# The chunked recurrence with its inverse in two halves and the turned inverse made by transposes

## The reference, cut to what matters

```python
def wkv7_scan(state0, r, w, k, v, a_vec, b_vec, reverse):
    def step(S, inp):
        r_t, w_t, k_t, v_t, a_t, b_t = inp
        sa = jnp.einsum('bhij,bhj->bhi', S, a_t)
        S = (S * w_t[:, :, None, :] + sa[..., None] * b_t[:, :, None, :]
             + v_t[..., None] * k_t[:, :, None, :])
        return S, jnp.einsum('bhij,bhj->bhi', S, r_t)
```

## Time and profile before

| | before |
|---|---|
| median of 3 runs | 2858.52 us (2855.38 to 2859.93) |
| profiled execution | 2863.22 us |
| its span, first to last instruction | 2861.4 us |
| PE busy, of the span | 2508.4 us (88%) |
| DVE busy | 1637.7 us (57%) |
| ACT busy | 1215.2 us (42%) |
| POOL busy | 426.4 us (15%) |
| mean granted TensorE clock | 0.930 |

### The profile page before, as it was taken

How to read it: one execution, slowest core, us unless ns; L and a number is a source line. 1 busy time by engine, 2 the same in 40 slices (tenths; PEclk the granted TensorE clock), 3 DMA queues, 4 the chain that set the end, 5 groups by cost and what they waited for, 6 DMA issues and landing times.

```text
span 2861.4 us, 55427 instructions
## 1 busy us (share of the span) xinstructions
PE 2508.4 (88%) x23264; PEld 1945.2 (68%) x23264; DVE 1637.7 (57%) x2360; ACT 1215.2 (42%) x1740; POOL 426.4 (15%) x412
## 2 busy tenths in 40 slices
PE   6979889999978779997888887899977889988996
PEld 5745577787857436785888765777766656767774
DVE  3655535555442274445566564588965355548895
ACT  2433333222231216424333324278864247446784
POOL 1010001000010020002455401122220030012221
PEclk9978989999999779998999988999988899999997
DMA  4246922222211000100000031199863100017995
GB/s 176 89 154 254 351 87 96 96 88 97 93 61 45 25 0 1 78 16 5 2 0 0 10 139 61 68 385 378 339 263 133 66 1 2 25 70 286 355 345 199
DMA packets 63892, 353.33 MB, mean 123 GB/s; under 512 B 15329, under 2 KB 15345, under 8 KB 27248
## 3 DMA queue, kind: packets, MB, share of 16 engines
q1 hardware_dynamic: 41792, 292.60, 26.9%
q0 software_dynamic: 21936, 58.50, 5.5%
HBM read 344.91 MB, written 36.70 MB: 133 GB/s over the span
## 4 chain that ended last, share of the span: by engine, by line
PE 72%; DVE 8%; ACT 5%; issue 4%; PEld 3%; DVEq 3%; DMA 2%; POOL 1%; POOLq 1%; ACTq 1%; PEldq 1%
PE psum L642 13%; PE psum L436 12%; PE psum L3271 9%; PE psum L3293 4%; PE psum L1187 4%; PE psum L1827 3%; PE psum L1206 3%; PE psum L1197 3%; PE psum L2882 2%; PEld psum L436 2%; PE psum L2232 2%; PE psum L1733 2%; PE psum L2211 1%; PE psum L3236 1%; PE psum L1045 1%
## 5 line engine op out<-in xcount | busy, mean ns | idle before, releaser
L436 PE MATMUL psum<-arena_r 128*128 128x512 f32 (+1 forms) x976 | 312.3, 361 | 4.3 <-DVE weight_slots_r L462 4.2
L642 PE MATMUL psum<-arena_r 128*128 128x512 f32 x704 | 250.8, 397 | 10.8 <-issue 4.0
L436 PE MATMUL psum<-arena_r,weight_slots_r 128*128 128x512 f32 (+1 forms) x696 | 249.1, 358 | 0.0
L457 ACT ACTIVATE arena_r<-weight_slots 128x1024 fp32r<-128x1024 f32 x73 | 76.4, 1057 | 334.5 <-PE psum L436 251.1
L642 PE MATMUL psum<-arena_r,weight_slots_r 128*128 128x512 f32 x528 | 209.1, 396 | 0.0
L436 PEld LDWEIGHTS psum<-arena_r 128*128 128x128 f32 x976 | 179.3, 190 | 36.0 <-issue 4.3
L436 PE MATMUL psum<-h_t_r,arena_r 128*128 128x512 f32 (+1 forms) x528 | 192.7, 365 | 0.0
L3225 DVE TENSOR_TENSOR weight_slots_r<-weight_slots,arena_r 128x2048 fp32r<-128x2048 f32 x78 | 177.6, 2290 | 20.1 <-ACT arena_r L3220 19.7
L3225 DVE TENSOR_TENSOR weight_slots_r<-weight_slots,h_t_r 128x2048 fp32r<-128x2048 f32 x72 | 163.9, 2290 | 20.9 <-ACT h_t_r L3220 20.8
L642 PEld LDWEIGHTS psum<-arena_r 128*128 128x128 f32 x704 | 133.8, 190 | 45.6 <-issue 13.6
L1271 DVE TENSOR_REDUCE stat<-psum 128x1 f32<-128x768 f32 (+1 forms) x112 | 98.7, 881 | 108.1 <-PE psum L1187 107.9
(11 more groups left out here) (469 smaller groups left out, 5485.0 us busy)
## 6 DMA issues: line engine op xcount, KB each, us to landing
weight_slots<-in_weights SPq DMA_DIRECT2D x277, 1024.0 KB, 6.8
arena<-y_rows POOLq DMA_DIRECT2D x20, 512.0 KB, 7.9
h_rows<-arena POOLq DMA_DIRECT2D x10, 512.0 KB, 2.9
x_keep<-x_t POOLq DMA_DIRECT2D x1, 3072.0 KB, 9.0
x_t<-x_keep POOLq DMA_DIRECT2D x2, 1536.0 KB, 8.6
x_t<-in_x POOLq DMA_DIRECT2D x1, 2048.0 KB, 9.8
out_x<-x_t SPq DMA_DIRECT2D x1, 2048.0 KB, 7.2
arena<-in_toe POOLq DMA_DIRECT2D x1, 1792.0 KB, 7.3
```

The lines of the kernel that those rows point to most:

```text
L436: last = self.nc.tensor.matmul(self.bank(n), w[:, kt, :], self.operand(part, kt, a, b), start=(i == 0), stop=(i == len(passes) - 1))
L642: last = nc.tensor.matmul(bank, w(p, k), x(q, k), start=(k == j == 0), stop=(k == n - 1 and j == 2))
```

## The change

The inverse is made in two halves, units c = 0, 1 and c = 2, 3, each with two banks of its own (4 and 5, 6 and 7). At each level and for each half PE first transposes x as it stands, two 128x128 transposes into the second half of the half's first bank (`turned`), and then makes the half product as before. ACT copies both out, the product to t1 and the transpose to xt, 128x256 each. Then come the products beside, then the growing of the first and of the second half; DVE adds each half to x. xt is no longer grown from level to level, only in the last level, where the growing is turned. So the turned set of grams, its preset and its mask (`up`) are gone.

The transposes of v, b and k and the key products move from the step's start into the levels: `key_grams` beside level 0, the last grams and the transposes of b and v beside level 1, `w_from_state` beside level 2, `w_from_keys` in one part and the transposes of k beside level 3, `y_from_state` beside level 4. ACT's copies of those transposes move behind levels 1 and 3. On DVE `reading` moves behind `low`, `removal` ahead of the adds of level 3, `new_keys` behind level 2, and the last mask behind level 1. On POOL `keyed` stands one level later. The units also lie in another, plainer arrangement, in which `w_from_state` and `y_from_state` and the last growing have their results in the same half as their operands.

The diff, cut to PE's levels, ACT, DVE and POOL:

```diff
-            wait("more_factors", n)
-            turn(6, w.vc)
-            turn(7, w.bt)
-            wait("y_added", n, -1)
-            turn(0, w.kt)
-            wait("masked", n, 2)
-            wait("read", n)
-            key_grams().then_inc(self.sem("more_grams"), 1)
-            for lv in range(self.LEVELS):
-                half(lv)
...
+            def half(lv, h):
+                for c in (2 * h, 2 * h + 1):
+                    for e, d in corners:
+                        last = t.matmul(into(4 + 2 * h, 0, d, c % 2, e), self.by_token(w.lo[lv % 2], c, d, e), self.by_token(w.x, c, d, e),
+                                        start=True, stop=True)
...
+            def turned(h):
+                for c in (0, 1):
+                    at = (2 * h + c) * P
+                    t.transpose(self.turned_bank(h)[:, c * P:(c + 1) * P], w.x[:, at:at + P], ident)
+            def grow(lv, h):
+                wait("level_half_copied", n, 2 * lv + h)
...
+            def beside(lv):
                 if lv == 0:
+                    wait("more_factors", n)
+                    wait("read", n)
+                    wait("state", n, -2)
+                    key_grams().then_inc(self.sem("more_grams"), 1)
+                if lv == 1:
+                    wait("y_added", n, -1)
+                    last_gram().then_inc(self.sem("more_grams"), 1)
+                    wait("more_masked", n, 0)
+                    turn(3, w.bt)
+                    turn(2, w.vc)
+                if lv == 2:
+                    w_from_state()
+                if lv == 3:
+                    w_from_keys()
+                    turn(2, w.kt)
+                if lv == last_lv:
+                    y_from_state()
+            for lv in range(self.LEVELS):
+                wait("level_blocks", n, lv)
+                for h in self.HALVES:
+                    if lv:
+                        wait("level_added", n, 2 * lv - 2 + h)
+                    turned(h)
+                    half(lv, h)
+                beside(lv)
+                for h in self.HALVES:
+                    grow(lv, h)
...
+        def half_copied(n, lv, h):
+            act.wait_ge(*self.at("level_half", n, 2 * lv + h))
+            s.activation(self.four(w.t1[:, self.cols(h)]), self.chain(h), ACT.Copy)
+            s.activation(w.xt[:, self.cols(h)], self.turned_bank(h), ACT.Copy).then_inc(self.sem("level_half_copied"), 1)
...
+        def grown(n, lv, h):
+            dve.wait_ge(*self.at("level_summed", n, 2 * lv + h))
+            if lv < self.LEVELS - 1:
+                x = self.four(w.x[:, self.cols(h)])
+                last = v.tensor_tensor(out=x, in0=x, in1=self.chain(h), op=ALU.add)
+            else:
+                x = w.xt[:, self.cols(h)]
+                last = v.tensor_tensor(out=x, in0=x, in1=self.turned_bank(h), op=ALU.add)
+            last.then_inc(self.sem("level_added"), 1)
...
+            key_masks(n)
             for lv in range(self.LEVELS):
+                if lv == 3 and more:
+                    removal(n + 1)
+                for h in self.HALVES:
+                    grown(n, lv, h)
+                if lv == 1:
+                    last_mask(n)
+                if lv == 2 and more:
+                    new_keys(n + 1)
                 if lv == 3 and more:
                     replacement(n + 1)
             if more:
...
                 low(n + 1)
-                new_keys(n + 1)
-                up(n + 1)
+                reading(n + 1)
             state(n)
...
-                if lv == 2 and n + 1 < self.STEPS:
+                if lv == 3 and n + 1 < self.STEPS:
                     keyed(n + 1)
             if n + 1 < self.STEPS:
-                preset_plain(n + 1)
-                preset_turned(n + 1)
+                preset(n + 1)
                 more_factors(n + 1)
```

More of the change, by code:

```diff
@@ L2201, in wait, with first_grams @@
             pe.reg_add(due[name], due[name], following - i)
+        def first_grams(n, ahead):
+            wait("factors", n, ahead)
+            gram(0).then_inc(self.sem("grams"), 1)
+            gram(1).then_inc(self.sem("grams"), 1)
         def step(n, more):
[L2204 to L2209, removed]
-                for c, e, d in units:
-                    last = t.matmul(bank_of(6, d, c, e, self.home(c, d)), self.plain(w.lo[lv % 2], c, e, d), self.plain(w.x, c, e, d),
-                                    start=True, stop=True)
-                last.then_inc(self.sem("level_half"), 1)
@@ L2215, in ready @@
-            def ready(lv):
-                wait("level_half_copied", n, lv)
-                if lv:
-                    wait("level_added", n, self.sum_of(lv - 1, 1))
-                else:
-                    wait("state", n, -2)
-            def grow(lv):
-                for c, e, d in units:
-                    last = t.matmul(bank_of(4, self.home(c, d), c, e, d), self.turned(w.xt, c, e, d), self.turned(w.t1, c, e, d),
-                                    start=True, stop=True)
-                last.then_inc(self.sem("level_summed"), 1)
@@ L2303, in step @@
             if more:
+                wait("token_rows", n, 2)
                 first_grams(n, 1)
-            wait("level_added", n, self.sum_of(last_lv, 1))
-            for c, e, d in units:
-                last = t.matmul(bank_of(6, self.home(c, d), c, e, d), self.turned(w.xt, c, e, d), self.turned(w.wv, c, e, d),
-                                start=True, stop=True)
-            last.then_inc(self.sem("u_summed"), 1)
-            if more:
-                turned_gram().then_inc(self.sem("grams"), 1)
@@ L2319, in step @@
+            last.then_inc(self.sem("solve_summed"), 1)
+            wait("solve_summed", n, 2)
             for c in range(4):
                 for e, d in corners:
-                    last = t.matmul(s_of(c, e, d), self.token_rows(w.br, c, e, d), self.plain(w.uv, c, e, d), start=False, stop=(c == 3))
+                    t.matmul(y_of(c, d, e), self.by_token(w.vr, c, d, e), self.by_token(w.rkt, c, d, e), start=False, stop=False)
+            if more:
+                wait("masked", n, 3)
+            else:
+                wait("token_rows", n, 2)
@@ L2322, in step @@
+            for c in range(4):
+                for e, d in corners:
+                    t.matmul(s_of(c, d, e), self.by_token(w.kr, c, d, e), self.by_token(w.vr, c, d, e), start=(c == 0), stop=False)
+            wait("solve_copied", n, 1)
+            for c in range(4):
+                for e, d in corners:
+                    last = t.matmul(s_of(c, d, e), self.by_token(w.br, c, d, e), self.by_token(w.uv, c, d, e), start=False, stop=(c == 3))
             last.then_inc(self.sem("state_summed"), 1)
@@ L2417, in replacement @@
             dve.drain().then_inc(self.sem("factors"), 1)
-        def mask(i, dst, m):
-            return v.tensor_tensor(out=self.four(dst), in0=self.by_head(*self.GRAMS[i]), in1=spread(m), op=ALU.mult)
         def low(n):
@@ L2489, in step @@
             decayed(n)
-        dve.wait_ge(*self.at("exps", 0))
-        for d in (0, 1):
-            removal(0, d)
-            reading(0, d)
-        dve.drain().then_inc(self.sem("read"), 1)
+        removal(0)
+        reading(0)
         replacement(0)
```

271 lines of the change are left out of this document (110 added, 161 removed).

## The result

| | before | after |
|---|---|---|
| median | 2859.22 us (4 runs) | 2886.55 us (4 runs, 2879.34 to 2896.13) |
| ratio | | 1.0099, interval 1.0065 to 1.0132 |
| profiled execution | 2863.22 us | 2883.44 us |
| its span | 2861.4 us | 2881.3 us |
| first to last key products of the recurrence | 260.5 us | 281.7 us (L2149 loads 1359.4, and 1641.1 in the last step) |

The change makes the kernel slower by 1.0%. Between the two profiled executions the difference is 20.2 us, and between its first and last key products the recurrence alone shows 21.2. From its first grams to the next stage's first product it takes 315.2 us (1352.87 to 1668.09) instead of 291.7, so 23.6 longer: the loss lies in it, and what is left outside, 3.4 us the other way, is less than executions of the kernel before differ by. The medians are further apart, 27.3 us.

The account below looks back on a forecast made before the run. In the recurrence, PE was taken to wait for a chain of hand-overs, not for itself. Steps -0.5, first step -1 and clock falls +4.5 make +3 on 2858.5: 2861.5 us; own range 2854 to 2869, 8 in 10 2843 to 2878.

Parts of the forecast that it names:

- From the state product to level 1: Recurrence step, state product's loads to level 1: 5.65 us instead of 7.28, with DVE's queue what is late.
- Levels 1 to 4: Recurrence step, level 1 to the end of level 4: 14.55 us instead of 12.22, so 2.3 more.
- Grams to state product: Recurrence step, first grams to state product: 3.13 us instead of 3.76, as reading stands behind.
- rival 1: PE's switches between whole-array and 64-wide products cost under 0.17: 2845 us at 0.10, 2829 at zero; chance 0.20.
- rival 3: Waits on PE's queue show between short groups: 0.05 for some 20 a step, +12, 2873 us; chance 0.12.
- Rival 4: One half waits for the other in the levels: at most +0.3 a level; no chance of its own given.
- The clock: PE's idle time before level 1, some 1.8 us, makes the clock fall in three steps at 1.5: +4.5 us.
- rival 2: The clock falls in every step: eleven falls at 1.7 to 2.2, +19 to +24, 2878 to 2882 us; chance 0.18.
- The first step: Recurrence's first step, no longer with transposes and POOL ahead of level 0: -1 us, bounds 0 and -1.6.
- -0.5: Recurrence's twelve steps, from the walk of one step: about -0.05 us a step, -0.5 over twelve.

Follow-up runs that it names:

- both edits: Changed kernel with the reading products ahead of the low masks and POOL's third block product held behind the decay: 2867.46 us, 1.0027.
- the growings apart: Changed kernel with reading ahead of the low masks; in levels 1 to 3 the first half's growing ahead of the products beside: 2866.05 us, 1.0016.
- the first block held: Changed kernel, DVE's order kept, with POOL's first block product of a step waiting until reading is done: 2863.01 us, 1.0021.
- the third block held: Changed kernel with POOL's third block product of a step waiting for the decay of the state: 2863.17 us, 1.0014.

## Why the prediction was wrong, point by point

- **From the state product to level 1** is the step that failed: 5.65 forecast, 7.42 measured. The walk let the state's add start 0.72 behind its product and took the decay at 0.94. Measured, the add starts 1.96 behind (1484.56 to 1486.52), since two reading products of 2.51 us stand before it, and the decay takes 1.72: both wait for POOL's block products. I had noted that POOL's first block "can start after the first mask", and that reading now stands behind the masks, but priced neither beside the other; nor did I see that the 0.94 was itself a decay beside POOL. (The terms of 5.65 as written add up to 5.57.) With reading ahead of the masks the term measures 5.71 (L2295 at 1495.86 to 1501.57).
- **Levels 1 to 4**: 14.55 forecast, 14.20 measured, level by level within 0.11. **Grams to state product**: 3.13 and 3.26. With reading first the three terms are 5.71, 14.20 and 3.49, together 23.40 against the forecast's 23.33. That this comes so close is partly luck: in an order that the walk did not have, the levels are 0.35 short and the last term 0.36 long.
- **Switches** (rival 1): 0.17 idle ahead of each half product. The other way shows no idle load, but the transposes come 0.39 behind a half product (1492.35 to 1492.74) whose eight products take 0.23, so some 0.16. Rival 1 is out; its price was off too, as 20 switches of 0.17 are 3.4 a step and not 2.7. **Waits on PE's queue** (rival 3) don't show: L2156 follows a half product with no idle load. Rival 4 is out too: the second half waits nowhere in the levels.
- **The clock** (rival 2): 1.5 per fall was right, three falls were too few; there were six. Idle time was forecast at 1.8 and is 3.2. The rival was to decide "from about six falls", so by its own mark it came in half; its eleven falls at 1.7 to 2.2 did not. The Trainium skill, TensorE: Matmul & The Clock Gate, section Part 4: PE-mode transpose, was weighed as a reason for falls; with 32 transposes a step and the idle time filled there was none (1.00 above), so they are not enough for one; whether they count less is not shown.
- **The first step** gained 3.3 (24.38 for 27.68) where I took 1 and set 1.6 as the bound. Before, the fall of the earlier trace rows lies in it; after, none does.
- In the sum: ten steps 1.60 longer without falls are 16, the falls 8 to 9, the first step -3; that is the 21 us of the stage. The forecast of +3 had -0.5, 4.5 and -1 there. The range ended at 2878 because none of its cases had a slower DVE.

What stays open: what decides whether a given idle time makes the clock fall. The same 0.91 of 4 us did so in every second step only; 1.66 us of idle time gave three falls with reading first, four with both edits, five with the growings apart and two with the first block held, and 2.18 gave none with the third block held (1502.78 in its trace). Where 1.1 to 1.3 us were left there was none. And only one execution of each kernel was traced: the changed kernel's two slower times have the lower clock, but where it fell in them isn't shown.

## What to carry to other kernels

Before pricing a moved DVE instruction by its old duration, look whether both its operands lie in SBUF and what POOL starts just ahead of it at the new place: the same product took 0.42 or 1.3 us. Where an idle time ahead of a short chain can't be removed, put work that is due later into it; here 0.46 us of it paid twice, in the level that it left and in the clock.

## What the runs showed of the hardware

- DVE beside POOL: a DVE product of 128x512 with two SBUF operands that ran into a POOL product ended 0.54 us behind it in three traces (0.82 to 1.72 us, where it takes 0.69 alone). Where the DVE product started ahead, POOL's was longer (1.43 for 1.27). Two in a row against two of POOL's took 2.51 us instead of 0.75.
- The clock can be held with three instructions: three products of 512 columns in the idle time (3.21 us, 1.12 left) took all falls away, and the ratio to the kernel before from 1.0099 to 1.0047.
- PE's loop: with 80 more products in its body, PE idled 4.4 to 5.1 us at every second return to the loop's head, beside transfers on the instruction queue. The trace has 876 loads and as many products in a step of the kernel before, which shows none of this, and 896 in that run. The Trainium skill, Runtime: NRT & Kernel Launch, section Instruction fetch mechanics, says that a taken branch to code no longer held must wait for it to be fetched by DMA; the rows of every second return agree, but why the others pass and where the limit lies no run here shows.
